# Fifteen seven-product groups in place of twelve, with all plain down products in one row behind them

## The reference

```python
q = (xc @ w_query).reshape(-1, 8, 2, 128)
s1, s2 = (einsum('thd,hkd->thk', q[:, :, i], sub_keys[:, i]) for i in range(2))
v1, i1 = top_k(s1, 16); v2, i2 = top_k(s2, 16)
cand = v1[..., :, None] + v2[..., None, :]          # 256 candidates per head
cidx = i1[..., :, None] * 128 + i2[..., None, :]    # of 16384 experts
sv, pos = top_k(cand, 16); eidx = take_along_axis(cidx, pos)
w = softmax(sv) * gelu(einsum('thkd,td->thk', u_tab[eidx], xc))
y = einsum('thk,thkd->td', w, v_tab[eidx])
x = layer_norm(alpha * x + y)
```

## Time and profile before

| what | value |
|---|---|
| median of 3 runs | 3717.69 us (3717.36 to 3717.88) |
| the profiled execution's own time | 3718.94 us |
| its span in the trace | 3716.7 us |
| PE busy | 3671.4 us (99%), 18336 products |
| PE weight load busy | 3032.3 us (82%) |
| DVE busy | 2526.1 us (68%) |
| ACT busy | 1150.8 us (31%) |
| POOL busy | 2498.0 us (67%) |
| DMA | 555.03 MB, mean 149 GB/s |

### The profile page before, as it was taken

One profiled execution on the slowest core, in us unless ns is written; L12 is line 12 of the kernel. 1 busy time (PEld: TensorE's weight loads), 2 busy tenths in 40 slices (PEclk: granted clock), 3 DMA queues, 4 the chain that ended last, 5 costly groups with the idle time before them and its releaser, 6 DMA issues.

```text
span 3716.7 us, 53645 instructions
## 1 busy us (share of the span) xinstructions
PE 3671.4 (99%) x18336; PEld 3032.3 (82%) x18336; DVE 2526.1 (68%) x4281; ACT 1150.8 (31%) x1725; POOL 2498.0 (67%) x1124
## 2 busy tenths in 40 slices
PE   8999999999999999999999999999999999999998
PEld 7778888888888888888887788888888888888886
DVE  7545999994777555555675469999857775555546
ACT  1651134541111134444125412344511111444431
POOL 6445554336777699999764455543377776999995
PEclk9999999999999999999999999999999999999999
DMA  4122245886545433333221223368865553334332
GB/s 154 69 69 103 103 144 176 244 247 247 206 183 192 158 125 113 130 148 117 91 104 69 80 92 113 139 192 243 245 244 191 195 200 136 114 133 148 113 124 79
DMA packets 230084, 555.03 MB, mean 149 GB/s; under 512 B 10048, under 2 KB 141376, under 8 KB 181440
## 3 DMA queue, kind: packets, MB, share of 16 engines
q1 hardware_dynamic: 47968, 337.14, 25.6%
q10 hardware_dynamic: 181984, 216.17, 17.3%
HBM read 446.32 MB, written 106.95 MB: 149 GB/s over the span
## 4 chain that ended last, share of the span: by engine, by line
PE 94%; DVE 3%; POOL 2%; issue 1%; ACT 0%; DMA 0%; POOLq 0%; DVEq 0%; ACTq 0%
PE bank L1561 29%; PE bank L1562 29%; PE bank L1563 29%; PE bank L1890 2%; PE bank L1891 2%; POOL part_l L506 1%; PE bank L1687 1%; PE bank L1850 1%; PE bank L1675 1%; POOL part_h L518 1%; DVE X L1013 1%; DVE X L1015 1%; PE bank L1666 0%; PE bank L1667 0%; DVE stats L999 0%
## 5 line engine op out<-in xcount | busy, mean ns | idle before, releaser
L506 POOL TENSOR_TENSOR part_l<-landing,part_h 128x1024 fp32r<-128x1024 f32 x536 | 1414.6, 2646 | 531.4 <-ACT part_h L766 454.7
L1561 PE MATMUL bank<-XTh,part_h 128*128 128x512 f32 (+1 forms) x2688 | 1047.4, 390 | 5.3 <-ACT Gf L661 2.9
L1563 PE MATMUL bank<-XTh,part_l 128*128 128x512 f32 (+1 forms) x2688 | 1034.1, 385 | 0.0
L1562 PE MATMUL bank<-XTl,part_h 128*128 128x512 f32 (+1 forms) x2688 | 1034.0, 385 | 0.0
L518 POOL TENSOR_SCALAR part_h<-landing 128x1024 fp32r<-128x1024 f32 x316 | 418.1, 1323 | 598.1 <-PE bank L1563 456.5
L1561 PEld LDWEIGHTS bank<-XTh,part_h 128*128 128x128 f32 x2688 | 505.2, 188 | 104.1 <-ACT Gf L661 3.8
L1563 PEld LDWEIGHTS bank<-XTh,part_l 128*128 128x128 f32 x2688 | 505.1, 188 | 101.6
L1562 PEld LDWEIGHTS bank<-XTl,part_h 128*128 128x128 f32 x2688 | 505.6, 188 | 95.5
L552 POOL TENSOR_TENSOR part_l<-vraw,part_h 128x1024 fp32r<-128x1024 f32 x168 | 420.4, 2529 | 42.7 <-ACT part_h L897 42.7
L1561 PE MATMUL bank<-part_h,Wh 128*128 128x512 f32 x1152 | 448.1, 389 | 0.0
L1562 PE MATMUL bank<-part_l,Wh 128*128 128x512 f32 x1152 | 448.1, 389 | 0.0
(11 more groups left out here) (214 smaller groups left out, 5904.0 us busy)
## 6 DMA issues: line engine op xcount, KB each, us to landing
landing<-stream SPq DMA_DIRECT2D x268, 1024.0 KB, 4.8
dense_gates<-spill ACTq DMA_DIRECT2D x32, 2048.0 KB, 9.3
gate<-dense_gates ACTq DMA_DIRECT2D x64, 1024.0 KB, 5.1
vraw<-stream SPq DMA_DIRECT2D x48, 1024.0 KB, 5.1
early_acts<-early ACTq DMA_DIRECT2D x144, 256.0 KB, 2.5
acts_in<-early_acts ACTq DMA_DIRECT2D x36, 1024.0 KB, 7.5
LNP<-ln ACTq DMA_DIRECT2D x4, 1024.0 KB, 5.9
X<-x SPq DMA_DIRECT2D x4, 512.0 KB, 7.3
```

Source lines behind the costliest of these rows:

```text
L506: nc.gpsimd.tensor_tensor(halves(part_l[s], h), halves(landing[s], h), halves(part_h[s], h).bitcast(F32), ALU.subtract).then_inc(split.sem, 1)
L1561: nc.tensor.matmul(dst, sth, mvh, start=first, stop=False)
L1562: nc.tensor.matmul(dst, sth, mvl, start=False, stop=False)
L1563: return nc.tensor.matmul(dst, stl, mvh, start=False, stop=last)
```

## The change

EG falls from 18 to 16 and E_AFTER goes, so that all 32 early pieces lie before or within the dense gates. SG rises from 12 to 15, and the only other late group is computed with the plain ones. The order of a layer's last stage becomes: up part of group 16 (its pieces are the last two that ACT and POOL split within the dense gates); fifteen seven-product groups (16 to 30), beside which the up part of group 31 is made as well; then all 17 plain down groups in one row: 31, 15, 0, 1, ... 14. The last of these is computed in `BLOCK_ORDER`. TensorE, DVE and ACT number the plain groups from 0 in this row.

ACT multiplies X by ALPHA in four operations after the last spill. DVE sets the accumulators to zero at the start of the stage. The eight additions of `gather_seven` are spread: two behind the work on each of the plain groups 0 to 3 of the row. Within a plain half the token halves come in the order 1, 0. SP loads the first table pieces of the seven-product stage when the spill has been stored. Some tiles move to other addresses.

```diff
-EG = 18
-E_BEFORE, E_AFTER = 16, 4
-E_WITHIN = 2 * EG - E_BEFORE - E_AFTER
+EG = 16
+E_BEFORE = 16
+E_WITHIN = 2 * EG - E_BEFORE
...
-SG = NG - EG - 2
+SG = NG - EG - 1
+S_UP = P_TAB + 2 * EG
...
@@ SP
-                sp.wait_ge(used.sem, used.at(l, P_UV))
-                down_piece(0, 0)
-                up_piece(0, 0)
-                down_piece(0, 1)
-                up_piece(0, 1)
+                for s in range(2):
+                    plain_piece(S_UP, s, P_UV + 2 * s)
+                for s in range(2):
+                    up_piece(0, s)
+                for s in range(2):
+                    sp.wait_ge(spilled[s].sem, spilled[s].at(l, 16 * (S // 64)))
+                for s in range(2):
+                    down_piece(0, s)
...
@@ ACT
+                act.dma_start(gate[0][:], dense[EG]).then_inc(gate_in[0].sem, 16)
+                for slot in range(4):
+                    act.wait_ge(early_saved[slot].sem, early_saved[slot].at(l, 16 * EG))
+                for tb in range(TB):
+                    ins = nc.scalar.activation(X[:, tb, :], X[:, tb, :], ACT.Copy, scale=ALPHA)
+                ins.then_inc(scaled.sem, 1)
...
                 for p in range(2):
                     activate(0, 2 * p, None)
-                    activate(0, 2 * p + 1, P_UV + 2 * p + 1)
+                    activate(0, 2 * p + 1, S_UP + p + 1)
+                    if p == 0:
+                        for h in range(2):
+                            up_high(0, 0, h, (used.sem, used.at(l, S_UP + 1)))
                     raw_highs(0, 0, p)
                     sum_highs(0, p)
                 fetch(EG + 1, 0, False)
...
@@ DVE
-                def gather_seven():
+                def gather_seven(group, steps):
...
+                    dve.wait_ge(seven_added.sem, seven_added.at(l, 7 * SG))
+                    dve.wait_ge(y_added.sem, y_added.at(l, 4 * group + 4))
+                    for n in steps:
+                        dst, new = [(p6, p1), (p7, p6), (x11, p1), (x12, p6), (x21, p7), (x22, p7), (x12, p5),
+                                    (x22, p5)][n]
+                        if n > 0:
+                            dve.wait_ge(acc_step.sem, acc_step.at(l, n))
                         nc.vector.tensor_tensor(dst, dst, new, ALU.add).then_inc(acc_step.sem, 1)
...
+                    dve.wait_ge(acc_step.sem, acc_step.at(l, steps[-1] + 1))
+                    dve.sem_inc(went_on, 1)
...
+                seven_group(SG - 1, 0, True)
+                dve_group(0, 0, (v_low.sem, v_low.at(l, 7 * SG)))
+                gather_seven(0, (0, 1))
+                dve_group(1, 1, (used.sem, used.at(l, S_DOWN + 2)))
+                gather_seven(1, (2, 3))
+                for q in (2, 3):
+                    dve_group(q, q - 2, (used.sem, used.at(l, S_DOWN + 2 * q)))
+                    gather_seven(q, (2 * q, 2 * q + 1))
+                with dve.Fori(2, EG // 2) as m:
+                    for par in range(2):
+                        dve_group(2 * m + par, par, (used.sem, used.at(l, 4 * m + (S_DOWN + 2 * par))))
...
@@ PE
-                for i in range(E_AFTER):
-                    for j in range(2 * KD):
-                        early_product(E_BEFORE + E_WITHIN + i, 0, j, False)
...
-                    for s in range(2):
+                    for n, s in enumerate((1, 0)):
...
-                down_group(0, 0, P_VA, [])
-                with pe.Fori(0, EG // 2 - 1) as m:
-                    down_group(2 * m + 1, 1, 4 * m + (P_VA + 2))
-                    down_group(2 * m + 2, 0, 4 * m + (P_VA + 4))
-                pe.wait_ge(early_out.sem, early_out.at(l, CG * EG))
-                both_group(EG - 1, Wh[:, 1], Wl[:, 1], P_UV, lambda c: (w_low.sem, w_low.at(l, CG * (EG - 1) + c + 1)))
+                for half in range(2):
+                    up(half, S_UP + half, half, lambda c: (early_out.sem, early_out.at(l, CG * EG)))
                 with pe.Fori(0, SG // 2) as m:
                     for par in range(2):
                         seven_group(2 * m + par, par)
-                both_group(EG, end_h[0], end_l[0], S_UV, lambda c: (w_low.sem, w_low.at(l, CG * EG + c + 1)),
-                           [(seven_added.sem, seven_added.at(l, 7 * SG))])
+                seven_group(SG - 1, 0)
+                down_group(0, end_h, end_l, [(seven_added.sem, seven_added.at(l, 7 * SG - 1 + n)) for n in range(2)])
+                down_group(1, Wh[0], Wl[0])
+                with pe.Fori(1, EG // 2) as m:
+                    for par in (1, 0):
+                        down_group(2 * m + (1 - par), Wh[par], Wl[par])
```

More of the change, by code:

```diff
@@ L440, in _, with rounds @@
                     sp.dma_start(C[:], consts).then_inc(const_in, 16)
-            def rounds(first, end, sevens):
+            def rounds(first, end, ahead):
                 with sp.Fori(first, end) as r:
                     for s in range(LANDINGS):
-                        sp.wait_ge(split.sem, r * (2 * LANDINGS) + 2 * (s - LANDINGS + 1 - 2 * SG * sevens))
+                        sp.wait_ge(split.sem, r * (2 * LANDINGS) + 2 * (s - LANDINGS + 1 + ahead))
                         sp.dma_start(landing[s][:], flat[r * LANDINGS + s]).then_inc(landed[s], 16)
@@ L614, in xt_parts @@
                                    bank[banks[i]][:].rearrange("p (k t) -> p k t", k=4)).then_inc(xt_high.sem, 1)
+            for k in range(2):
+                act.sem_inc(spilled[k].sem, 16)
             root(1, slice(0, 2))
@@ L828, in early_half @@
                     early_gelu(4 * b + (2 * E_BEFORE + c), ready, (left, slot))
-                gate_block(0, True)
-                with act.Fori(1, S // 64) as b:
-                    gate_block(b, False)
+                with act.Fori(0, S // 64) as b:
+                    gate_block(b)
                 for k in range(2):
                     act.wait_ge(spilled[k].sem, spilled[k].at(l, 16 * (S // 64)))
[L835 to L846, removed]
+                act.dma_start(gate[0][:], dense[EG]).then_inc(gate_in[0].sem, 16)
[4 more added lines that the diff above has]
+                ins.then_inc(scaled.sem, 1)
                 def fetch(g, par, acts_too):
@@ L853, in fetch, with down_highs @@
                                       ).then_inc(acts_back[par].sem, 16)
[L855 to L862, removed]
+                def down_highs(q, par, tile_free, next_group):
+                    act.wait_ge(*tile_free)
+                    for c in range(CG):
+                        act.wait_ge(w_full.sem, w_full.at(l, CG * q + (CG * (NG - EG) + c + 1)))
+                        nc.scalar.copy(Wh[par][:, c, :], bank[c][:]).then_inc(w_high.sem, 1)
+                    if next_group is not None:
+                        fetch(next_group, par, True)
                 def activate(a, c, piece_done):
@@ L1503, in _ @@
-                dve.wait_ge(gate_in[0].sem, gate_in[0].at(l, 16))
-                dve.wait_ge(acts_back[0].sem, acts_back[0].at(l, 16))
-                weigh(0, 0, 0, W_FIRST)
-                weigh(0, 0, 1, W_FIRST)
-                dve.wait_ge(early_out.sem, early_out.at(l, CG * EG))
-                dve_group(1, 1, None, lambda half: P_VA + half + 1)
-                with dve.Fori(1, EG // 2) as m:
-                    for par in range(2):
-                        dve_group(2 * m + par, par, 4 * m + (2 * par + P_VA - 2),
-                                  lambda half: 4 * m + (2 * par + P_VA - 1 + half))
@@ L1515, in _ @@
+                    dve.wait_ge(acc_step.sem, acc_step.at(l, steps[-1] + 1))
+                    dve.sem_inc(went_on, 1)
+                for k in range(2):
+                    dve.wait_ge(spilled[k].sem, spilled[k].at(l, 16 * (S // 64)))
+                for i in range(4):
+                    ins = nc.vector.memset(acc[i][:], 0.0)
+                ins.then_inc(acc_zero.sem, 1)
                 for p in range(2):
@@ L1961, in seven_products @@
                             if i in UNIT_RAW:
[L1962 removed]
+                                wh, wl = (w[par][:, UNIT_RAW[i], a, ts] for w in (raw_h, raw_l))
                             else:
```

236 lines of the change are left out of this document (97 added, 139 removed).

## The result

The changed kernel takes **3753.03 us** (median of 4 runs, 3751.34 to 3755.95) against 3717.53 (4 runs, 3716.99 to 3717.88): a ratio of 1.0096, 95% interval 1.0079 to 1.0114, so 35.5 us slower where 24 were forecast. The profiled execution took 3753.36 us, its span is 3751.6, with a mean granted clock of 0.994.

The account below looks back on a forecast made before the run. TensorE was taken to bound the kernel, in steady parts by its number of matmuls. The terms -16.3 - 0.6 + 26.4 + 13.4 + 1.1 = +24.0 us on 3717.7 gave 3742 us, range 3722 to 3753.

Parts of the forecast that it names:

- Matmuls: Three more groups per layer take seven products instead of eight: 72 matmuls fewer at 0.2265 us, -16.3 us.
- old wait of 0.3 us: Behind the last seven-product group, TensorE's wait for POOL's second piece, some 0.3 us per layer, goes: -0.6 us.
- 0.55 us at the first plain piece: End of the seven-product groups: the piece's second half is ready late, 0.55 us per layer, +1.1 us.
- The additions: Plain groups 1 to 4, half boundary: TensorE waits 3.3 us for DVE's delayed work, eight times, +26.4 us.
- written-out sequence of DVE and POOL: Plain half: two-SBUF-input DVE operations and POOL's alternate; second weighing ends at 11.40 us, X additions at 14.0, against 10.7 due.
- E: Plain rhythm: the addition at 1007.34, from which the half's later operations are counted; it lies 0.2 us behind a boundary.
- clock falls in the start's idle stretch: Rival: the clock falls at the seven-product groups' start, 3.4 us per layer, time 3748; chance 0.09.
- The start: Start of the seven-product groups: TensorE waits 6.7 us per layer in all, +13.4 us, bounds 5.0 and 8.3.
- G: Start of the seven-product groups: the gate tile lands between 860.3 and 863.6; the middle, 862, was taken.
- The forecast's split: Start of the seven-product groups: 1.2 us wait for banks, about 4.3 us idle in one stretch before the third product.
- the additions are hidden, wholly or by half: Rivals at plain groups: wholly hidden, 3715, chance 0.13, or 3704 with short start, 0.06; about half hidden, 3729, 0.06.
- 2.88 us of idle: DVE's idle time in each plain half; it lets DVE catch up in the other half, so nothing carries over.

Follow-up runs that it names:

- experiment 4: Changed kernel, but SP holds back the first two table pieces of the seven-product stage until the gate tile has landed: 3746.61 us.
- experiment 1: Changed kernel without the eight additions per layer that bring the accumulators into X: 3721.66 us.
- experiment 2: Changed kernel with all eight additions made one per half, behind the half's first X addition, where DVE idles: 3721.25 us.
- experiment 5: Changed kernel, but ACT makes the first table unit's two casts ahead of the second pair's weight casts: 3742.97 us.
- experiment 8: Changed kernel with additions in idle stretches, gate tile before table pieces, ACT's table casts earlier, and first up piece waiting per bank for its own GELU: 3704.27 us.

## Why the prediction was right or wrong

The direction came true, and so did the forecast's mechanisms for the additions and the start; the falls of the clock, to which it gave nothing, are missing from its sum. The size was short by 11.5 us, and the time lies 0.03 us above the top of the range.

- *Matmuls* (-16.3): 72 fewer, as forecast. The old wait of 0.3 us (-0.6) is gone too, and the 0.55 us at the first plain piece came as forecast. The old waits of 0.6 us in the last group, gone as well (-1.2), were not in the forecast.
- *The additions* (+26.4): right in place, number and mechanism, 3.0 us instead of 3.3 each, +24.0. The written-out sequence of DVE and POOL happened as it stood but for its end, 10.9 us behind E where 11.4 was worked out. The wait for the additions was so much the forecast's core that a second thing in the same place was missed: **"clock falls in the start's idle stretch"** was given as a rival with a chance of 0.09 and a price of 3.4 us per layer, and for the gather waits not considered at all. Four of those eight waits have a fall behind them.
- *The clock* is **the failed step**. The argument against the rival was that no clock falls behind the few shorter waits of the kernel before; the new waits are longer, and they were weighed by those instead of by the earlier trace rows, where a mostly idle stretch was followed by 0.51. Each fall lasts 3.41 us and costs 1.7 us. Six of the eight add to the time, 10.2 us, where the forecast had nothing and the rival 6.8: it priced a fall at twice what one cost, and looked for them in one place of two. The 10.2 us are most of the miss of 11.5. The errors of the additions (-2.4) and of the start (+2.4) cancel, which is luck.
- *The start* (+13.4): the mis-sized term was the landing of the gate tile, G. DVE starts on it at 864.16, beyond the upper bound of 863.6 and 2.2 behind the 862 that was taken. Of these 0.6 is the issue, at 855.79 instead of 855.22, and 1.6 the way: 8.4 us, where 6.8 was taken and the upper bound had 8.4. The chain behind it took 26.0 us instead of 26.7. So TensorE is delayed 7.9 us per layer instead of 6.7, **+15.8** for +13.4. It is split otherwise, too: 3.0 at the banks and 2.3 at the third product, with a fall between them, instead of 1.2 and 4.3. The forecast's split, one long wait, would have had one fall in a layer, as experiment 4 has; there are two, of which the first hides in the chain.

The busy time by stretch shows the DMA engines full while the tile is on its way in the changed kernel, and not in experiment 4. The third row is of the kernel before:

```profile
856.00:861.00 5.00, 5.00 (x24) 4.14 (x23) 3.65 (x4) 4.60 (x6) 0.00 (x0) 1.00 0.99 385
861.00:864.00 3.00, 3.00 (x15) 2.50 (x14) 0.00 (x0) 2.18 (x3) 1.69 (x1) 1.00 1.00 423
```

```profile
856.00:861.00 5.00, 5.00 (x23) 4.13 (x22) 3.72 (x5) 4.71 (x6) 0.00 (x0) 1.00 0.74 279
```

```profile
855.00:861.00 6.00, 6.00 (x28) 4.95 (x28) 0.00 (x0) 1.75 (x3) 5.65 (x4) 1.00 0.98 369
```

Full engines alone don't make the tile late. In the kernel before they were as full (0.98), and the tile, issued at 855.22, was there within the usual 5.1 us: apart from the rest of a piece that SP had issued at 851.40, what was fetched beside it stood behind it in ACT's own queue, from 855.61 on. The changed kernel has that older piece too (851.33), and in addition the two table pieces from SP's queue, the first issued in the same moment as the tile, at 855.79.

The Trainium skill, "DMA: Bandwidth & Descriptors" (Queues, rings and completion order), has each DMA engine take packets from the queues in turn. The tile's 8.4 us beside another queue's two pieces, against 5.2 without them, agree with that.

- *The rivals*: that the additions are hidden, wholly or by half, is refuted by their eight waits and by experiment 1. That they could be hidden is shown by experiment 2: the 2.88 us of idle that the forecast used only to say that nothing carries over was room for one of them in each half.

## What to carry to other kernels

Price a wait of the bounding engine twice, once for its length and once for the clock behind it: here eight of twelve waits of 2.3 us or more were followed by a fall that costs 1.7 us, of which six added to the time, and those of 1 us or less by none, so shortening a wait can gain more than its length. Put an extra operation where its engine already idles, not ahead of the next thing that someone waits for; the same eight additions cost 31 us in one place and nothing in the other. And when a stage is moved, count again which transfers of other queues now run beside the one that its first step waits for.

## What was not expected of the hardware

Waits of nearly the same length differ in what comes behind them. Counted over the profiles of the changed kernel and of all eight experiments, in the stages from the dense gates to the last plain group: all waits up to 1.04 us had no fall behind them; of the waits of the start of 2.3 us and more, 22 of 23 had one; of those of 3.0 us in the plain groups, 13 of 24. In experiment 5, for one:

```profile
1520.00:1524.00 4.00, 3.85 (x17) 3.22 (x18) 4.00 (x4) 0.59 (x1) 3.92 (x3) 1.00 0.00 0
1545.00:1549.00 4.00, 3.99 (x11) 3.11 (x12) 4.00 (x4) 0.59 (x1) 3.92 (x3) 0.59 0.01 4
1571.00:1575.00 4.00, 3.52 (x11) 2.86 (x12) 4.00 (x5) 0.59 (x1) 3.92 (x3) 0.75 0.02 4
1598.00:1602.00 4.00, 4.00 (x18) 3.31 (x19) 4.00 (x4) 0.59 (x1) 3.92 (x3) 1.00 0.00 0
```

The second and third of the four waits have a fall behind them, the first and fourth none, though they are 3.0 to 3.1 us each; in layer 0 of the changed kernel it was the first and the third, in its layer 1 the second and the third. Why one wait has it and another not stays open. It may be a source of spread, but that isn't shown, as only one execution of each version was profiled: the changed kernel's four runs differ by 4.6 us, and its two slowest have the lower mean clock (0.994 against 0.995), while the five runs of experiment 8, whose profile has no such fall, differ by 1.4.
